# Routing tables of a two-layer mixture-of-experts step: ranks on TensorE, a 16-block slot table first, overflow and gate weights after the first gather

## What is computed

```python
_, g_idx = lax.top_k(g_logits, 1)                    # 1 of 4 groups
top_v, top_i = lax.top_k(e_logits, TOP_K)            # 2 of 8 experts in the group
weights = (p_grp * jax.nn.softmax(top_v, axis=-1))
expert_idx = g_idx * EXPERTS_PER_GROUP + top_i
y = (silu(xb @ wg[e]) * (xb @ wu[e])) @ wd[e]        # per token and chosen expert
out = sum over the two choices of weight * y
```

## Time and profile before, and how to read it

| What | us |
|---|---|
| median of 3 runs | 1384.5 |
| the profiled execution, its own time | 1380.93 |
| its span in the profile | 1379.2 |
| PE busy | 1173.4 (85%) |
| DVE busy | 706.6 (51%) |
| ACT busy | 280.2 (20%) |
| POOL busy | 106.9 (8%) |

### The profile page before, as it was taken

The page is one execution under the profiler, slowest core; times in us unless marked ns, Lnnn a source line. Parts: engine busy times, 40 slices in busy tenths (PEclk is TensorE's granted clock), DMA queues, the critical chain, the costliest instruction groups (busy, mean ns, idle before and its releaser), DMA issues.

```text
span 1379.2 us, 20219 instructions
## 1 busy us (share of the span) xinstructions
PE 1173.4 (85%) x7522; PEld 661.8 (48%) x7522; DVE 706.6 (51%) x1625; ACT 280.2 (20%) x700; POOL 106.9 (8%) x163
## 2 busy tenths in 40 slices
PE   5999999889986787987859999988899589689681
PEld 3555544554552444554424555555445355356440
DVE  3355877785376231332362687877754732233224
ACT  1210043662111000000022013347312110000000
POOL 2000000001001110110000000000100021111100
PEclk9999999999988998999989999999999589899996
DMA  9311101248459999999960211015573489999996
GB/s 375 161 69 58 62 31 39 93 168 319 171 192 388 415 420 420 418 418 420 410 260 14 85 59 61 1 62 191 203 318 134 177 351 418 419 419 420 419 400 245
DMA packets 59762, 334.58 MB, mean 243 GB/s; under 512 B 10672, under 2 KB 10672, under 8 KB 27404
## 3 DMA queue, kind: packets, MB, share of 16 engines
q1 hardware_dynamic: 45216, 295.78, 52.9%
q0 software_dynamic: 14448, 37.50, 7.1%
HBM read 320.31 MB, written 25.51 MB: 251 GB/s over the span
## 4 chain that ended last, share of the span: by engine, by line
PE 48%; DMA 17%; SPq 14%; DVE 9%; issue 5%; ACT 3%; DVEq 2%; PEld 2%; POOL 0%; ACTq 0%; PEldq 0%; POOLq 0%
PE bank L1762 13%; SPq L389 11%; PE bank L2061 10%; PE bank L1693 9%; DMA ring<-in_stream 8%; DMA U<-in_stream 5%; PE bank L2178 3%; PE bank L2211 3%; SPq L387 2%; DVE U L1276 2%; DMA CAT<-moe_in,tabs 1%; PE bank L2077 1%; DMA U<-moe_out 1%; PE bank L1850 1%; PE bank L1876 1%
## 5 line engine op out<-in xcount | busy, mean ns | idle before, releaser
L1762 PE MATMUL bank<-HT,ring 128*128 128x512 f32 (+1 forms) x640 | 175.4, 435 | 2.1 <-issue 2.1
L2178 PE MATMUL bank<-U,HT 128*32 128x256 f32 (+2 forms) x992 | 150.8, 410 | 24.8 <-DMA ring<-in_stream 12.1
L2178 PE MATMUL bank<-ring,HT 128*32 128x256 f32 (+2 forms) x800 | 139.8, 415 | 34.8 <-DMA U<-in_stream 25.2
L1693 PE MATMUL bank<-ring,HT 128*128 128x512 f32 x320 | 148.3, 605 | 2.9 <-ACT HT L658 1.4
L1762 PEld LDWEIGHTS bank<-HT,ring 128*128 128x128 f32 x640 | 97.3, 191 | 79.8 <-issue 79.8
L2178 PEld LDWEIGHTS bank<-U,HT 128*32 128x32 f32 (+2 forms) x992 | 87.1, 135 | 62.8 <-issue 42.7
L1119 DVE SCALAR_TENSOR_TENSOR U<-U,prm 128x655 f32<-128x655 f32 x120 | 107.9, 899 | 7.7 <-issue 0.4
L2061 PE MATMUL bank<-ring,HT 128*128 128x512 f32 x240 | 106.3, 592 | 0.0
L2178 PEld LDWEIGHTS bank<-ring,HT 128*32 128x32 f32 (+2 forms) x800 | 76.8, 136 | 61.0 <-issue 44.6
L1555 DVE TENSOR_TENSOR HT<-bank,HT 128x256 f32<-128x256 f32 x32 | 13.6, 424 | 177.0 <-ACT HT L888 177.0
L888 ACT ACTIVATE HT<-bank 128x256 f32<-128x256 f32 x32 | 12.3, 383 | 412.5 <-PE bank L2178 412.5
(11 more groups left out here) (372 smaller groups left out, 1693.1 us busy)
## 6 DMA issues: line engine op xcount, KB each, us to landing
ring<-in_stream SPq DMA_DIRECT2D x142, 1024.0 KB
U<-in_stream SPq DMA_DIRECT2D x72, 1024.0 KB, 26.2
spare<-in_stream SPq DMA_DIRECT2D x24, 1024.0 KB, 25.4
RAB<-in_stream SPq DMA_DIRECT2D x14, 1024.0 KB
U<-moe_out SPq DMA_DIRECT2D x20, 512.0 KB, 8.1
U<-in_stream SPq DMA_DIRECT2D x14, 512.0 KB
CAT<-in_stream SPq DMA_DIRECT2D x14, 512.0 KB
RAB<-mod_rows POOLq DMA_DIRECT2D x12, 512.0 KB, 7.7
```

Source lines behind the costliest of these rows:

```text
L1693: ins = e.matmul(bank[:], HT[:, k, t * P:(t + 1) * P], wide(q, k), start=(k == 0), stop=(k == KD - 1))
L1762: ins = e.matmul(out, wt(q)[:, k, P * (n % 2):P * (n % 2) + P], HT[:, k, lo:lo + w], start=(k == 0), stop=(k == KD - 1))
L2178: ins = e.matmul(PS[2 + p][s, FF * j:FF * j + FF], xgT[:, p, k, s], w, start=(k == 0), stop=(k == KD - 1))
```

## The change

The ranks are counted on TensorE. Five more matmuls give each expert's count down the partitions (`keycol`), one comparison of 32 elements gives who stands above whom (`above`), and one matmul by ones sums it (second count of `rank_ps`, now two per layer). The slot table has only the 16 main blocks (32 columns instead of 70), its one-hot of places is made in two halves, each with its own `chosen`, and TensorE begins with the first half; five matmuls of 16 columns give which slots hold a second choice (`slot_ps` counts to two per layer). A slot past the capacity is pushed off the 16 blocks by adding 4096 (`rk3`). The list of the gather comes from one copy and one operation. The overflow scan stands behind that list, the overflow's slots, the float32 table of places and the weights' table in `late_tables`, behind the copy of round 0's rows and ahead of `gated(0)`; what TensorE makes of them, ten matmul calls of 54 columns behind `rows_in(1)`, is read in `late_slots`. SyncE waits for `slot_ps` alone before tiles 14 and 15. At most 3 chunks instead of 4 stand ahead of the slot table (first layer only; the second has 2). At the start VectorE waits for all constants and does two small operations before it fills the banks, and GpSimd makes two index columns and a masked column more. The core of the diff:

```diff
         def before_slots(l):
 
-            return min(4, modd(l) // 2)
+            return min(3, modd(l) // 2)
...
-                e.wait_ge(S["tables_rdy"], 3 * l + 3)
-                e.wait_ge(S["wslot_ps"], l + 1)
+                e.wait_ge(S["slot_ps"], 2 * (l + 1))
                 for i in range(SPLIT + 1, PLACES - 1):
...
+                e.wait_ge(S["tables_rdy"], 3 * l + 3)
                 some = e.value_load(ovn[0:1, 0:1], min_val=0, max_val=NOVF)
...
+            e.iota(rowp, [[0, 1]], base=0, channel_multiplier=1, allow_small_or_imprecise_dtypes=True)
+            e.iota(keyadd, [[0, 1]], base=0, channel_multiplier=-1, allow_small_or_imprecise_dtypes=True)
+            e.memset(keymul, float(NE))
+            e.drain()
+            e.affine_select(out=keymul, in_=keymul, compare_op=ALU.is_ge, fill=0.0, base=-FIXED, pattern=[[0, 1]], channel_multiplier=1)
             e.iota(spread[:], [[32, 4], [1, 8], [8, 4]], base=0, channel_multiplier=0, allow_small_or_imprecise_dtypes=True).then_inc(c, 1)
...
+            e.wait_ge(S["cst"], 24)
+            e.tensor_scalar(small(1600, 1), keymul, -1e6 / NE, 1e6, ALU.mult, ALU.add)
+            dr()
+            e.tensor_tensor(keyadd, keyadd, small(1600, 1), ALU.add)
             for j in range(2):
                 ins = e.memset(PS[4 + j][:], 0.0)
             ins.then_inc(S["silu_c"], 1)
...
-                                       op0=ALU.mult, op1=ALU.subtract); dr()
-                over = mt[:, 1, :].rearrange("p (e f) -> p e f", e=NE)
-                e.tensor_tensor(over, key.unsqueeze(1).to_broadcast((P, NE, NE)), key.unsqueeze(2).to_broadcast((P, NE, NE)), ALU.is_gt); dr()
-                e.tensor_reduce(rank, over, AX, ALU.add); dr()
...
+                e.wait_ge(S["rank_ps"], 2 * l + 1)
+                e.scalar_tensor_tensor(out=key[:, FIXED:], in0=counts[:, FIXED:], scalar=float(NE), in1=iota[:, FIXED:NE],
+                                       op0=ALU.mult, op1=ALU.subtract)
+                e.tensor_scalar(keycol[0:NE], PS[6][0:NE, NE * (NT + 1):NE * (NT + 1) + 1], keymul[0:NE], keyadd[0:NE], ALU.mult, ALU.add); dr()
+                e.tensor_scalar(above[0:NE], key[0:NE], keycol[0:NE], None, ALU.is_lt).then_inc(S["chosen"], 1)
+                e.tensor_copy(rk, PS[6][:, 0:NT * NE].rearrange("p (t n) -> p t n", t=NT))
+                e.tensor_copy(cnt, counts)
+                e.wait_ge(S["rank_ps"], 2 * l + 2)
+                rank, ranked = PS[7][:, 0:NE], small(1452, NE)
+                e.tensor_copy(ranked, rank)
+                e.tensor_scalar(base2, rank, float(BIGS), float(2 * QUART), ALU.min, ALU.mult)
+                e.tensor_scalar(beside, rank, float(3 * QUART), float(QUART * (3 - 4 * BESIDE - 3 * BIGS - MIDS)), ALU.mult, ALU.add)
                 e.tensor_scalar(capm, rank, float(BIGS), float(HALF), ALU.is_lt, ALU.mult)
...
                 e.tensor_copy(lanes, lane).then_inc(S["tables_rdy"], 1)
-                e.tensor_scalar(at0, at0, float(QUART), None, ALU.mult)
+                e.tensor_tensor(rk, rk, at0.unsqueeze(1).to_broadcast(bc), ALU.add); dr()
+                e.scalar_tensor_tensor(out=rk3, in0=late, scalar=4096.0, in1=rk, op0=ALU.mult, op1=ALU.add); dr()
+
...
+                slots_of(rk3, U[:, LATER + 2 * D:LATER + 2 * D + 2 * NT * NE])
+                main = (P, 2 * NT, NR)
+                e.tensor_tensor(block16, iota[:, 0:NR].unsqueeze(1).to_broadcast(main), blk10.unsqueeze(2).to_broadcast(main), ALU.is_equal); dr()
+                e.tensor_scalar(rows16[:, :, 0, :], block16, rowp, None, ALU.mult)
+                e.tensor_tensor(rows16[:, :, 1, :], block16, rowhi.unsqueeze(2).to_broadcast(main), ALU.mult)
+                places(place16, 0, NT).then_inc(S["chosen"], 1)
+                places(place16, NT, 2 * NT).then_inc(S["chosen"], 1)
...
+                first = PS[6][:, 0:NR]
+                e.wait_ge(S["slot_ps"], 2 * l + 1)
+                e.tensor_copy(sf2[:, 0:NR], PS[6][:, NR:2 * NR]); dr()
+                e.scalar_tensor_tensor(out=gidx[:, 0:NR], in0=first, scalar=2048.0, in1=sf2[:, 0:NR], op0=ALU.add, op1=ALU.add
+                                       ).then_inc(S["tables_rdy"], 1)
+                e.scalar_tensor_tensor(out=sf[:, 0:NR], in0=first, scalar=2048.0, in1=sf2[:, 0:NR], op0=ALU.add, op1=ALU.add)
                 e.tensor_scalar(step, step, 0.0, None, ALU.max); dr()
-                e.tensor_copy(novi, step); dr()
+                e.tensor_copy(novi, step)
+                e.wait_ge(S["slot_ps"], 2 * (l + 1))
+                e.scalar_tensor_tensor(out=slots[:, 0:NR], in0=PS[7][:, 0:NR], scalar=float(NTOK), in1=sf[:, 0:NR], op0=ALU.mult, op1=ALU.add)
...
-                e.tensor_tensor(place16, spread[:].unsqueeze(1).to_broadcast((P, 2 * NT, P)),
-                                small(160, 2 * NT).unsqueeze(2).to_broadcast((P, 2 * NT, P)), ALU.is_equal)
-                e.tensor_tensor(blockno, iota[:, 0:NBLK].unsqueeze(1).to_broadcast((P, 2 * NT, NBLK)),
-                                small(170, 2 * NT).unsqueeze(2).to_broadcast((P, 2 * NT, NBLK)), ALU.is_equal); dr()
-                e.tensor_scalar(rows16[:, :, 0, :], blockno, rowno[:, 0, 0:1], None, ALU.mult)
-                e.tensor_tensor(rows16[:, :, 1, :], blockno, rowhi.unsqueeze(2).to_broadcast((P, 2 * NT, NBLK)),
-                                ALU.mult).then_inc(S["chosen"], 1)
...
-                e.wait_ge(S["slot_ps"], l + 1)
-                sf, sf2 = small(0, NBLK), small(50, NBLK)
...
-                e.tensor_copy(gidx, sf).then_inc(S["tables_rdy"], 1)
...
-                e.tensor_tensor(W2, W1, dx, ALU.mult); dr()
-                e.tensor_tensor(place, spread[:].unsqueeze(1).to_broadcast((P, 2 * NT, P)),
-                                small(160, 2 * NT).unsqueeze(2).to_broadcast((P, 2 * NT, P)), ALU.is_equal)
-                wblk = mt[:, 0, 0:2 * NT * NBLK].rearrange("p (j n) -> p j n", j=2 * NT)
-                e.scalar_tensor_tensor(out=wblk, in0=blockno, scalar=0.0, in1=small(1235, 2 * NT).unsqueeze(2).to_broadcast((P, 2 * NT, NBLK)),
-                                       op0=ALU.is_gt, op1=ALU.mult).then_inc(S["chosen"], 1)
...
+                e.tensor_tensor(W2, W1, dx, ALU.mult)
                 for j in range(modd(l) // 2):
                     modulation(l, j)
...
+                def late_tables():
+
...
+                    e.tensor_tensor(late, late, step.unsqueeze(1).to_broadcast(bc), ALU.mult)
...
+                    e.tensor_reduce(ovf[:, 1:], cmp, AX, ALU.add)
+                    e.tensor_tensor(rk, rk, late, ALU.add); dr()
...
+                    slots_of(rk, htf[:, 3 * D:3 * D + 2 * NT * NE])
+                    e.tensor_scalar(ovf[:, 1:], ovf[:, 1:], 3.0, float(experts(l)), ALU.mult, ALU.add); dr()
+                    every = (P, 2 * NT, NBLK)
+                    e.tensor_tensor(blockno, iota[:, 0:NBLK].unsqueeze(1).to_broadcast(every), blk10.unsqueeze(2).to_broadcast(every), ALU.is_equal); dr()
+                    e.tensor_tensor(wrows[:, :, 0:NBLK], blockno, small(1235, 2 * NT).unsqueeze(2).to_broadcast(every), ALU.mult)
+                    e.tensor_tensor(wrows[:, :, NBLK:], blockno[:, :, NR:], rowno.unsqueeze(2).to_broadcast((P, 2 * NT, NOVF)), ALU.mult)
+                    places(place, 0, 2 * NT).then_inc(S["chosen"], 1)
...
+                def late_slots():
+
+                    over, over2 = sf[:, NR:], sf2[:, NR:]
+                    e.wait_ge(S["wslot_ps"], l + 1)
+                    found = PS[7][:, NBLK:WIDE]
+                    e.tensor_copy(wslot, PS[7][:, 0:NBLK])
...
+                    e.tensor_copy(gidx[:, NR:], over)
+                    e.tensor_scalar(lat, sf, float(CTX), None, ALU.is_ge)
+                    e.tensor_copy(ovn, ovf)
+                    e.drain().then_inc(S["tables_rdy"], 1)
...
                 rows_in(0)
+                late_tables()
                 gated(0)
                 rows_in(1)
+                late_slots()
...
                 e.matmul(PS[6][:, NE * (NT - 1):NE * NT], triS[:], M16[:, NT - 1, :], start=False, stop=False, skip_group_check=True)
-                e.matmul(PS[6][:, NE * NT:NE * (NT + 1)], ones16[:].to_broadcast((P, P)), M16[:, NT - 1, :], start=False, stop=True, skip_group_check=True
-                         ).then_inc(S["rank_ps"], 1)
+                e.matmul(PS[6][:, NE * NT:NE * (NT + 1)], ones16[:].to_broadcast((P, P)), M16[:, NT - 1, :], start=False, stop=True, skip_group_check=True)
+                for j in range(NT):
+                    ins = e.matmul(PS[6][0:NE, NE * (NT + 1):NE * (NT + 1) + 1], M16[:, j, :], ones16[:], start=(j == 0), stop=(j == NT - 1),
+                                   skip_group_check=True)
+                ins.then_inc(S["rank_ps"], 1)
+                e.wait_ge(S["chosen"], 6 * l + 3)
+                above = small(0, NE // 2).bitcast(BF16)
```

(18 more changed lines are left out.)

141 lines of the change are left out of this document (65 added, 76 removed).

## The result

The changed kernel took 1372.8 us (median of 4 runs, 1367.9 to 1376.1), the kernel before 1384.4 us beside it (4 runs, 1384.0 to 1384.8): with a ratio of 0.9933 on record (95% interval 0.9905 to 0.9961; the two medians alone would give 0.9916). Three of these four executions of before are the three behind the 1384.5 us that the forecast started from. Forecast were 1377.4 us and a range of 1375.3 to 1380.3. The profiled execution was the slowest of its four: 1376.1 us, span 1374.3.

What follows compares the result with a forecast made beforehand. Transfers were taken to bound the expert stages, so only idle DMA time counted: 1.5 + 1.7 + 3.9 = 7.1 us off 1384.5 (profiled 1380.9 plus 3.6 carried over) gave 1377.4 us, range 1375.3 to 1380.3.

Steps and rivals of the forecast that it cites:

- the carry-over: The runs' median lay 3.6 us above the profiled execution of before; this was added to the forecast time.
- the sum: Idle DMA time removed around the routing in both layers: 1.5 + 1.7 + 3.9 = 7.1 us.
- the start: First weight tiles: constants end at 9.6 us, TensorE done with two tiles by 15.2; costs nothing, up to 1 us if later.
- What bounds the kernel: Expert stages end when their bytes are through; only removing time in which the DMA engines are idle pays.
- All of it counts: Rival: the chain runs through VectorE, so 8.7 us per layer come through, giving 1367.1 us; chance 0.04.
- Ranks and lanes: After the second layer's counts: lanes 1.7 us sooner, ending that much DMA idleness at 1076 to 1091 us.
- Reading ranks from PSUM: Seven VectorE operations read ranks from PSUM: nothing added; the skill page's estimate was 0.45 us more.
- SyncE: Second layer: seven ring tiles flow for 17.6 us from 1090.3; tile 16 is issued by 1106.5, before the engines run dry.
- place four: Second layer, 1106 to 1115 us, DMA share 0.57: 3.9 us of idleness, claimed to be filled.
- place two: First layer, 431 to 434 us, DMA share 0.50: 1.5 us of idleness, claimed to be removed.
- The gather: Second layer's first gather goes out 8.7 us sooner and may take 10.7 us; the median gather takes 8.4.
- late_tables: About 7.5 us of VectorE ahead of `gated(0)`, hidden beside round 0's gate and up matmuls of over 8.4 us.

Runs made afterwards that it cites:

- again: The changed kernel run once more, unaltered, for its spread: median 1372.9 us, ratio 0.9927 to the kernel before.
- again2: The changed kernel unaltered, run a further time in another group: median 1374.4 us, ratio 0.9933 to the kernel before.
- before_start: The kernel before with only the changed kernel's later start (one more memset and drain, VectorE waiting for all constants): median 1379.1 us, ratio 0.9980.
- tiles_wait: The changed kernel, but SyncE issues weight tiles 14 and 15 only when all the tables are there: median 1390.4 us, ratio 1.0042 to the kernel before.
- gather_late: The changed kernel, but GpSimd issues the first gather only when the modulation's first rows stand in SBUF: median 1377.0 us, ratio 0.9959 to the kernel before.
- ranks_dve: The changed kernel with its ranks found pairwise on VectorE again, as before the change: median 1375.7 us, ratio 0.9944 to the kernel before.
- start_undone: The changed kernel with the start of the kernel before: median 1374.5 us, ratio 0.9936 to the kernel before.

## Why the prediction was wrong in size, and where it was right

The forecast of 1377.4 us lay 4.6 us above the measured 1372.8. Against the means of all executions (54 of the kernel before in the later groups, 1382.1 us; 16 of the changed kernel, 1372.6) this is 2.4 us in the base and 2.4 us in the sum, within about 0.9 us, the standard error of the difference of these means.

**First step that failed: the carry-over.** The sum was made against the profiled execution, 1380.9 - 7.1 = 1373.8. Then 3.6 us were added, "The median of the runs lies 3.6 us above it and I carry that over". The three executions told nothing of the scatter: the later groups put the middle of the kernel before at 1382.1 us, 1.1 us above the profiled execution and not 3.6. The range of 1375.3 to 1380.3 had no term for it. Without the carry-over the forecast would have been 1373.8, close to what was measured, but by luck: a base 1.1 us too low and a sum 2.4 us too small cancel in part.

**Second: the sum was short.** It had 7.1 us; the means are 9.5 apart, the ratios of the result, `again` and `again2` give 9 to 10, and in the group of the result, where the kernel before did stand at 1384.4, 11.6 us came off. The idle time removed was right: idle 1 fell by 5.4 us (33.3 to 27.9; forecast 5.6), that of layer 0, added up in the same way, by 1.5 (15.7 to 14.2; forecast 1.5). The stretches of experts shrank by 6.7 and 2.0 us, but mixer 1 took 1.6 more, so behind the last choice of layer 0 the profiles give 7.0 us, the sum that was forecast. What is missing lies ahead of it or in the scatter.

**Third: the start**, priced at nothing with "four small operations at 0.29 or less". A drain stood between them and took 4 us. My threshold, "TensorE's first matmul pushing past 16 us at the third tile", was passed (18.25), which I had priced at up to 1 us of loss. It cost nothing by 20.4 us, since TensorE made it up without waiting for tiles. With the old start the changed kernel averaged 1373.9 us (12 executions) instead of 1372.6, and `before_start` stood 2.6 us below before in its group: so the later start is where 1.3 to 2.6 us of the missing 2.4 may be. The place of this gain was not found; it is not the start itself (65.3 against 64.7 us at the common point), and it stays open.

**Right, by the steps of the forecast.**
- *What bounds the kernel.* Borne out by tiles_wait, gather_late and ranks_dve: time follows idle transfers. "All of it counts" (1367.1) is refuted by layer 0, where the gather went out 9.0 us sooner (+20.0 before, +11.0 after) for a gain of 2.0, and where delaying it by 5.2 us cost 0.2.
- *Ranks and lanes.* Lanes 1.9 us sooner (1.7 forecast), list 8.9 us sooner (8.7), gather issued at +10.9 (before +19.8). The answer of TensorE to the single wait: `above` from 1086.52 to 1086.75, ranks read at 1087.03, so 0.2 and 0.3 us, as forecast.
- *Reading ranks from PSUM.* 0.18 to 0.19 us, 0.10 apart, like SBUF. The estimate from the Trainium skill (VectorE: DVE Perf Modes, section on the TRN2 errata) of 0.065 us more each was not seen.
- *SyncE.* Tile 16 at +22.7 (forecast +22.6), no dip at place four, none behind chunk 3 (place two).
- *The gather.* 8.2 us (1096.40 to 1104.60) with seven tiles issued ahead of it, and 6.3 before with a nearly empty queue. The Trainium skill (DMA: Bandwidth & Descriptors, Queues, rings and completion order) has the queues taking turns packet by packet; the trace agrees, since seven tiles of 2.5 us each, flowing from 1091.8, would have lasted to 1109.4 and the gather did not wait for them. The forecast's "the gather may take 10.7 us" put the limit of the first transposes at 1105.7 in the trace of before, 21.8 us behind the last choice. In gather_late they stood at +25.1, 3.3 us beyond it, and layer 1 lost 3.4: the limit is borne out by this one profile.
- *late_tables.* 7.3 us on VectorE (1107.18 to 1114.50; forecast 7.5), and `gated(0)` then waits 2.24 us more for ScalarE (1116.73). Hidden, as forecast.

## What to carry to other kernels

Before adding a gain to a median, ask how far single executions of that kernel lie apart; three executions that agree within 0.6 us stood 2.4 us off the middle of a scatter of 9 us. A single profiled execution is no better as a base; here it happened to lie nearer. Measure both ends of a sum by the same kind of number, and give the range a term for the scatter. Where transfers bound a stage, price a change by the holes in the DMA share, and follow each queue to the next thing it will wait for: removing one of two waits that end the same hole can only move it, as the early tiles did here. Behind such a change, put first in the critical engine's order the few operations that the next transfer waits for.

## What the hardware did that was not expected

- GpSimd's drain took 4.0 us at 5.6 us of the kernel and 1.05 us when it stood at 8.7 us (`start_undone`); in `before_start` it took 4.2 us at 5.5. All three ended at 9.6 to 9.7. The four DMA issues that began at 1.34 us are the likeliest earlier work of that engine to be still running; this was not tested.
- The same pause of TensorE was followed by a granted clock of 1.00 in one execution and of 0.66 in another of nearly the same program, and mixer 0 differed by up to 5 us between two executions of one program.
